# First attention: the steps of two heads placed between the matmuls of the following query blocks, and the query norm carried as one factor per token

## The chip, the cores and the metric

The kernel runs on one core of one Trainium2 chip. The metric is the device time of one execution in microseconds (us). Before the change it is 3598.67 us, the median of three runs (3596.43 to 3601.0). The profiled execution of the same kernel took 3606.35 us, with a span of 3604.6 us in the trace.

## The reference

The program is a stack of attention, recurrent and feed-forward blocks over 256 tokens of width 2048, all in float32. The change touches the first attention alone: 32 query heads and 8 key/value heads of width 64, a causal band of 128 keys, a sink per head.

```
qkv = h @ w_qkv
q, k, v = split(qkv)                       # 2048 + 512 + 512 columns
q = rmsnorm(q per head, q_gain)            # over 64 values of a head
k = rmsnorm(k per head, k_gain)
scores = einsum(q, k) * 64 ** -0.5
scores = where(0 <= qpos - kpos < 128, scores, min)
probs = softmax(concat([scores, sink]))[..., :-1]
out = einsum(probs, v)
x = x + out @ w_o
```

## The kernel before

Every weight product is cut into *units*. A unit makes a tile of 128 output features for 256 tokens: 16 steps over the 2048 input features, each with two matmuls. To keep float32 precision at the quick matmul rate, a weight tile is split into a rounded head (`w_head`, by ScalarE, L561) and the rest (`w_tail`, by VectorE, L837), and the activations are stored as head and rest side by side (`h`, 512 columns). The first matmul of a step multiplies the head of the weights with both halves (512 columns, L272), the second the tail of the weights with the heads (256 columns, L273). ScalarE copies the upper half of the bank into `lo` (L567), and VectorE adds it to the lower half (`product`, L843). A ring of four weight slots and two raw slots is filled by DMA on SyncE's queue, one tile of 1 MB a unit; the tile of unit u + 3 is split while unit u runs. Two banks, `unit0` and `unit1`, take turns.

The first attention has 24 units: 4 for keys (two heads to a tile), 4 for values, 16 for queries. In a query unit VectorE scales the product by the token norm `rstd`, ScalarE squares it, TensorE sums the squares over each head (`head_norm`, L289), ScalarE takes ln and exp for the inverse root (`head_root`, L576 and L577, each with a load of an activation table), VectorE refines it with one Newton step on 128x256 elements and writes the normed query tile to `store` (L986). The order of instructions on each engine is written out by hand, and semaphores join the engines; each engine takes its own list strictly in order.

After all 24 units the 32 heads run one by one (`attn_scores`, `attn_tile`, `turn_p`, `values`). For a head TensorE makes the scores of two blocks of 128 queries against 256 keys (L315), VectorE adds the mask (L880), takes the maximum over keys (L885) and the negative maximum with the sink (L889); ScalarE takes the exponentials with their sums (L604, L607); VectorE divides (L896 to L900); TensorE transposes four blocks (L326), ScalarE copies them (L613), TensorE multiplies by the values (L335). After each pair of heads VectorE writes the output tile, as head and rest, to `act` (L998, L999). Then the output product (`wo`, 16 units) starts; its first unit waits for all of `act`.

Of the kernel before, what the change touches and what calls it, by code (L numbers as in the profile page):

```python
# [70 lines left out]
OUTS = {"even_a": 0, "even_b": 8, "odd": 16}  # L71
NORMS = {"attn": 0, "even_kv": 20, "even_a": 22, "even_b": 30}
QS = {"attn": 0, "even_kv": 20, "even_a": 22, "even_b": 30, "odd": 38}
VTS = {"attn": 0, "even_kv": 4, "even_b": 6, "odd": 14}
# [6 lines left out]
GELUS = {"up00": 0, "up01": 16, "up02": 32, "lru_y": 48, "up10": 64, "up11": 80, "up12": 96}  # L81
GATES = {"even_a": 0, "even_b": 8, "odd": 16}
FINALS = ["wo", "down02", "lru_out", "down12", "even_out", "odd_out"]


def known(v):
    return isinstance(v, int)
# [30 lines left out]
def build(nc, t):  # L118

    ctx = ExitStack()  # L120
    with ctx:
        def sb(name, shape, dt=F32):
            return ctx.enter_context(nc.sbuf_tensor(name, shape, dt))
# [4 lines left out]
        def sem(name):  # L128
            return ctx.enter_context(nc.semaphore(name))
# [33 lines left out]
        rd = sb("rd", [P, 2, 2])  # L163
        lamb = sb("lamb", [P, 8])

        unit_bank = [pb("unit0"), pb("unit1")]
# [17 lines left out]
        p_done, t_mm, pt_done = sem("p_done"), sem("t_mm"), sem("pt_done")  # L184
        o_mm, o_read = sem("o_mm"), sem("o_read")
        gate_in, gate_th = sem("gate_in"), sem("gate_th")
        lru_a, lru_b, lru_c, lru_root, lru_d = (sem(n) for n in ("lru_a", "lru_b", "lru_c", "lru_root", "lru_d"))
# [71 lines left out]
        def _(pe):  # L259
# [89 lines left out]
            def residual(name):  # L349
                plain(name, act, (act_done, READY[name]))  # L350
# [31 lines left out]
            def trailing(g):  # L382
                if known(g) and RING <= g < 2 * RING:
                    return lambda: turn_v(g - RING, kv[:, g, :])
                n = g if known(g) and g < RING else g - RING
                return lambda: head_norm(n, halves)

            def project(i):
                for j in range(RING):
                    g = i * RING + j  # L390
                    if known(g) and g == 0:
                        first_unit()
                    else:
                        unit(i * RING + (BASE["attn"] + j), j, h, (trailing(i * RING + (j - 1)),))
            for i in range(3):
                project(i)
            with pe.Fori(3, UNITS["attn"] // RING) as i:
                project(i)
            trailing(UNITS["attn"] - 1)()


            def attn_scores(n):
                tile, lanes = n // 2, slice(HD * (n % 2), HD * (n % 2 + 1))
                scores(store[lanes, tile, :], kv[lanes, tile // 4, :], ps_s[n % 2], 20, (n - 1,) if n >= 2 else ())
            attn_scores(0)
            attn_scores(1)
            for n in range(N_Q):
                if n + 2 < N_Q:
                    attn_scores(n + 2)
                turn_p(n, n % 2)  # L410
                c = HD * (n % 2)
                values(n, ps_o[c:c + HD, 0:SEQ],
                       [kv[:, 4 + n // 8, kt * P + c:kt * P + c + HD] for kt in range(QT)], n // 2, act_done)
            residual("wo")
            ffn(0, 1)
# [136 lines left out]
        def _(a):  # L552
# [87 lines left out]

            def project(i):
                for j in range(RING):
                    u = i * RING + (BASE["attn"] + j)
                    if known(i) and i == 1:
                        step(u, j)
                        copy_vt(j, kv[:, 4 + j, :])
                    else:
                        n = i * RING + j if known(i) and i == 0 else i * RING + (j - 4)
                        step(u, j)
                        head_square(n, prod[:, :])  # L650
                        head_root(n, HD)
            project(0)
            project(1)
            repeat(a, 2, 6, project, chain)

            exps(0, 0, col(sinks, 0))

            def attn_tile(i):

                exps(i * 2 + 1, 1, col(sinks, i * 2 + 1))  # L660
                copy_pt(i * 2)
                if not (known(i) and i == N_Q // 2 - 1):
                    exps(i * 2 + 2, 0, col(sinks, i * 2 + 2))
                copy_pt(i * 2 + 1)
            repeat(a, 0, N_Q // 2 - 1, attn_tile)
            attn_tile(N_Q // 2 - 1)

# [161 lines left out]
        def _(v):  # L829
# [9 lines left out]

            def product(u, slot):  # L840

                v.wait_ge(lo_done, u + 1)
# [103 lines left out]
            v.tensor_scalar(hb[:, 1, :], lru[:, :, L_BI], 0.5, None, ALU.mult)  # L946
            v.tensor_scalar(dims[:, C_QG:C_QG + 1], dims[:, C_QG:C_QG + 1], HD ** -0.5, None, ALU.mult)
            v.tensor_scalar(dims[:, C_AQ:C_AQ + 1], dims[:, C_AQ:C_AQ + 1], HD2 ** -0.5, None, ALU.mult)
# [20 lines left out]

            def project(i):  # L970
                for j in range(RING):
                    u = i * RING + (BASE["attn"] + j)
                    product(u, j)
                    if known(i) and i == 1:
                        scaled(kv[:, 4 + j, :]).then_inc(vt_in, 1)
                        tail(u + LEAD, j + LEAD)
                        continue
                    k_tile = known(i) and i == 0
                    n = i * RING + j if k_tile else i * RING + (j - 4)
                    scaled(prod[:, :]).then_inc(norm_in, 1)  # L980
                    tail(u + LEAD, j + LEAD)
                    v.wait_ge(norm_rk, n + 1)
                    refine(rk[:, :], HD, EPS)
                    dst = kv[:, j, :] if k_tile else store[:, i * RING + (j - 8), :]
                    gain = C_KG if k_tile else C_QG
                    v.scalar_tensor_tensor(dst, prod[:, :], dims[:, gain:gain + 1], rk[:, :], ALU.mult, ALU.mult)\  # L986
                        .then_inc(q_done, 1)
                    v.wait_ge(q_done, n + 1)
            project(0)
            project(1)  # L990
            repeat(v, 2, 6, project, chain)

            def attn_front(n, slot, freed=None):
                front(n, slot, mask[:, :], 1.0, col(sinks, n), freed=freed)

            def attn_out(i):
                v.wait_ge(o_mm, i * 2 + 2)
                link(v.tensor_scalar(act[:, i, 0:SEQ], ps_o[:, 0:SEQ], 1.0, None, ALU.mult))  # L998
                v.tensor_tensor(act[:, i, SEQ:2 * SEQ], ps_o[:, 0:SEQ], act[:, i, 0:SEQ].bitcast(F32),  # L999
                                ALU.subtract).then_inc(act_done, 1)  # L1000

            def attn_tile(i, last=False):
                attn_front(i * 2 + 1, 1, None if known(i) and i == 0 else i * 2)
                back(i * 2, 0, True)
                if not (known(i) and i == 0):
                    attn_out(i - 1)
                if not last:
                    attn_front(i * 2 + 2, 0, i * 2 + 1)
                back(i * 2 + 1, 1, True)
            attn_front(0, 0)  # L1010
            attn_tile(0)
            repeat(v, 1, N_Q // 2 - 1, attn_tile, chain)
            attn_tile(N_Q // 2 - 1, True)
            attn_out(N_Q // 2 - 1)

# [82 lines left out]
            def lru_gate(m, u, slot, width, block_done):  # L1098
                v.wait_ge(lo_done, u + 1)
                v.tensor_tensor(kv[:, 7, :], act[:, m, 0:SEQ].bitcast(F32), act[:, m, SEQ:2 * SEQ].bitcast(F32),  # L1100
# [242 lines left out]
def constants():  # L1343

    q = (np.arange(QT)[None, :, None] * P + np.arange(P)[:, None, None])
    rel = q - np.arange(SEQ)[None, None, :]
    band = np.where((rel >= 0) & (rel < 128), 0.0, NEG)

# [35 lines left out]
```

## Time and profile before

| | |
|---|---|
| median of three runs | 3598.67 us |
| profiled execution | 3606.35 us, span 3604.6 us |
| TensorE busy | 3336.0 us, 93% of the span |
| VectorE busy | 2456.4 us, 68% |
| ScalarE busy | 1789.5 us, 50% |
| DMA | 561.11 MB, mean 156 GB/s |

Busy time is what the profiler saw between start and end of instructions. The granted clock tells how much of its full speed TensorE was allowed; at 0.5 a matmul of the same size takes about twice as long and is still counted busy. A busy share close to one is therefore no proof that nothing is to be gained in a stretch: the clock has to be read beside it. The chain of waits follows the work that ended last back through its releasers.

### The profile page before, as it was taken

To read this page: it belongs to the slowest core of one execution; us is meant where nothing else is said; L and a number is where in the kernel's file an instruction comes from. 1 tells how busy PE (TensorE), PEld (TensorE's weight loads), DVE (VectorE), ACT (ScalarE), POOL (GpSimd) and SP (SyncE) were. 2 spreads that over 40 slices of the span, in tenths; PEclk is the share of its full clock that TensorE was granted. 3 is DMA by queue.
4 is the path that set the end of the run, shared out by engine and by line. 5 is a ranking of instruction groups with operands and counts; after the bars stand their busy time and mean duration, and the time that the engine had idled before them with its cause. 6 is when DMAs were issued, how large, how long until landed. Compare 5 with 4: busy or idle time off the path is not lost.

```text
span 3604.6 us, 52426 instructions
## 1 busy us (share of the span) xinstructions
PE 3336.0 (93%) x17960; PEld 2820.0 (78%) x17960; DVE 2456.4 (68%) x3703; ACT 1789.5 (50%) x2281; POOL 13.1 (0%) x20
## 2 busy tenths in 40 slices
PE   8878999999999999769999999999778989999997
PEld 6744788888888888658888888888666777888876
DVE  6654577667667766777875775776455776666665
ACT  6843355445445445664554554554444554444443
POOL 1000000000000000000000000000000000000000
PEclk9965899999999999879999999999888999999998
DMA  5410355555555554235555555555223444445443
GB/s 186 144 43 0 105 186 187 181 187 184 182 187 186 182 180 150 95 117 176 197 186 187 186 179 186 185 184 186 105 84 105 152 149 141 174 164 175 173 146 122
DMA packets 83038, 561.11 MB, mean 156 GB/s; under 512 B 9728, under 2 KB 12800, under 8 KB 15872
## 3 DMA queue, kind: packets, MB, share of 16 engines
q1 hardware_dynamic: 82944, 559.87, 44.7%
q8 instruction: 57, 0.93, 0.1%
q14 instruction: 37, 0.30, 0.0%
HBM read 557.73 MB, written 2.10 MB: 155 GB/s over the span
## 4 chain that ended last, share of the span: by engine, by line
PE 70%; DVE 14%; issue 6%; ACT 6%; DMA 3%; DVEq 1%; ACTq 0%; SPq 0%
PE unit L272 42%; PE unit L273 21%; DVE w_tail L837 5%; PE o L335 2%; PE s L315 2%; PE tr L326 1%; DVE prod L843 1%; ACT w_head L561 1%; ACT L576 1%; DMA raw<-in_down 1%; ACT lo L567 1%; DMA raw<-in_lru_x 1%; ACT prt L613 1%; DVE mx L885 1%; DVE x L1024 0%
## 5 line engine op out<-in xcount | busy, mean ns | idle before, releaser
L272 PE MATMUL unit<-h,w_head 128*128 128x512 f32 x5808 | 2108.4, 406 | 40.1 <-DVE kv L1100 33.7
L273 PE MATMUL unit<-h,w_tail 128*128 128x256 f32 x5808 | 1643.3, 283 | 0.0
L272 PEld LDWEIGHTS unit<-h,w_head 128*128 128x128 f32 x5808 | 1110.9, 191 | 319.3 <-DVE kv L1100 37.0
L561 ACT ACTIVATE w_head<-raw 128x2048 fp32r<-128x2048 f32 (+1 forms) x540 | 1013.5, 1877 | 611.3 <-DMA raw<-in_up 210.8
L837 DVE TENSOR_TENSOR w_tail<-raw,w_head 128x2048 fp32r<-128x2048 f32 (+1 forms) x540 | 1209.5, 2240 | 11.5
L273 PEld LDWEIGHTS unit<-h,w_tail 128*128 128x128 f32 x5808 | 1115.4, 192 | 3.0
L272 PE MATMUL unit<-act,w_head 128*128 128x512 f32 x2560 | 910.7, 400 | 19.1 <-DVE act L854 12.9
L843 DVE TENSOR_TENSOR prod<-unit,lo 128x256 f32<-128x256 f32 x524 | 222.3, 424 | 756.2 <-ACT lo L567 750.4
L273 PE MATMUL unit<-act,w_tail 128*128 128x256 f32 x2560 | 720.6, 281 | 0.0
L272 PEld LDWEIGHTS unit<-act,w_head 128*128 128x128 f32 x2560 | 485.2, 190 | 140.6 <-DVE act L854 15.2
L273 PEld LDWEIGHTS unit<-act,w_tail 128*128 128x128 f32 x2560 | 487.7, 190 | 0.2
L567 ACT ACTIVATE lo<-unit 128x256 f32<-128x256 f32 x524 | 197.2, 376 | 316.2 <-PE unit L273 315.8
L691 ACT ACTIVATE kv<-kv,fconv 128x256 f32<-128x256 f32 x192 | 115.8, 603 | 187.3 <-DVE kv L849 187.3
L1045 DVE SCALAR_TENSOR_TENSOR kv<-kv,fconv 128x255 f32<-128x255 f32 (+1 forms) x384 | 184.8, 481 | 24.8 <-DVE kv L1045 0.9
L613 ACT ACTIVATE prt<-tr 128x512 f32<-128x512 f32 x64 | 38.3, 598 | 188.3 <-PE tr L326 188.3
L326 PE MATMUL tr<-ident,pr 128*128 128x128 f32 x256 | 59.4, 375 | 54.1 <-DVE pr L900 35.8
L607 ACT ACTIVATE pr<-pr,nm 128x256 f32<-128x256 f32 x144 | 71.5, 498 | 74.5 <-DVE nm L887 74.5
L849 DVE SCALAR_TENSOR_TENSOR kv<-prod,rstd 128x256 f32<-128x256 f32 x232 | 98.6, 425 | 9.0
L326 PEld LDWEIGHTS tr<-ident,pr 128*128 128x128 f32 x256 | 39.4, 188 | 82.5 <-DVE pr L900 41.5
L335 PE MATMUL o<-prt,kv 128*64 128x256 f32 (+1 forms) x160 | 72.3, 601 | 23.4 <-ACT prt L613 23.4
L587 ACT ACTIVATE sq<-x 128x256 f32 (+1 forms) x96 | 40.3, 419 | 107.9 <-DVE x L1024 107.9
L315 PE MATMUL s<-kv,store 64*128 64x256 f32 (+1 forms) x160 | 73.8, 622 | 9.9 <-DVE store L986 5.2
(157 smaller groups left out, 1610.4 us busy)
## 6 DMA issues: line engine op xcount, KB each, us to landing
raw<-in_up SPq DMA_DIRECT2D x192, 1024.0 KB, 4.9
raw<-in_down SPq DMA_DIRECT2D x96, 1024.0 KB, 4.9
raw<-in_odd SPq DMA_DIRECT2D x64, 1024.0 KB, 4.9
raw<-in_even_b SPq DMA_DIRECT2D x32, 1024.0 KB, 4.9
raw<-in_attn SPq DMA_DIRECT2D x24, 1024.0 KB, 4.9
raw<-in_wo SPq DMA_DIRECT2D x16, 1024.0 KB, 4.9
raw<-in_lru_y SPq DMA_DIRECT2D x16, 1024.0 KB, 4.9
raw<-in_lru_x SPq DMA_DIRECT2D x16, 1024.0 KB, 4.9
```

What stands on the lines that cost most here:

```text
L272: pe.matmul(bank[:, :], w_head[:, slot, at], src[:, k, :], start=k == 0, stop=False)
L273: last = pe.matmul(bank[:, 0:SEQ], w_tail[:, slot, at], src[:, k, 0:SEQ], start=False, stop=k == KT - 1)
L315: last = pe.matmul(bank[:, qt * SEQ:(qt + 1) * SEQ], q[:, qt * P:(qt + 1) * P], k, start=True, stop=True)
L326: last = pe.transpose(ps_t[:, kt * SEQ + qt * P:kt * SEQ + (qt + 1) * P], pr[:, slot, qt * SEQ + kt * P:qt * SEQ + (kt + 1) * P], ident[:, :])
L335: last = pe.matmul(out, v[kt], prt[:, kt * SEQ:(kt + 1) * SEQ], start=kt == 0, stop=kt == QT - 1)
L561: a.activation(w_head[:, slot, 0:width], raw[:, r, 0:width], ACT.Copy).then_inc(head_done, 1)
L567: a.activation(lo[:, slot % 2, :], unit_bank[slot % 2][:, SEQ:2 * SEQ], ACT.Copy).then_inc(lo_done, 1)
L691: a.activation(kv[:, 1 + j, :], kv[:, 0, :], ACT.Identity, scale=fconv[:, layer, tap, 2:3], bias=fconv[:, layer, tap, 3:4])\
L837: v.tensor_tensor(w_tail[:, slot, 0:width], raw[:, slot % 2, 0:width], w_head[:, slot, 0:width].bitcast(F32), ALU.subtract).then_inc(tail_ ...
L843: v.tensor_tensor(prod[:, :], unit_bank[slot % 2][:, 0:SEQ], lo[:, slot % 2, :], ALU.add)\
L849: return v.scalar_tensor_tensor(dst, prod[:, :], scale, rstd[:, :], ALU.mult, ALU.mult)
L1045: ins = v.scalar_tensor_tensor(y[:, back_by:SEQ], kv[:, 0, 0:SEQ - back_by], w, y[:, back_by:SEQ], ALU.mult, ALU.add)
```

## The change

The 4 key and 4 value units stay. Key tiles are now scaled by the product of both gains and -1/8, so that no gain has to be applied to the queries, and scores come out negated.

A query unit now has three matmuls of 256 columns a step, all into the same 256 columns of its bank (L468 to L470 of the changed kernel), so the sum of the parts needs no copy and no addition: VectorE takes the tile straight from PSUM, times `rstd` (`q_taken`, L1104). The query is not normed. Its squares are summed with the tokens on partitions, four columns for two blocks of tokens and two heads (`q_sums`), and the inverse root, 128x4 elements, multiplies the scores as one factor per token.

```diff
+            def q_part(t, k):
+                if k == 1 and t >= 2:
+                    q_turn(t - 2, 1)
+                if k == 2 and 1 <= t <= Q_TILES:
+                    q_sums(t - 1)
+                    q_scores(t - 1)
+                if k == 5 and t >= 2:
+                    q_values(t - 2)
+                if k == KT - 2 and 1 <= t <= Q_TILES:
+                    q_turn(t - 1, 0)
+            def q_unit(t):
...
+                for k in range(KT):
+                    pe.matmul(bank[:, 0:SEQ], w_head[:, slot, at], h[:, k, 0:SEQ], start=k == 0, stop=False)
+                    pe.matmul(bank[:, 0:SEQ], w_head[:, slot, at], h[:, k, SEQ:2 * SEQ], start=False, stop=False)
+                    last = pe.matmul(bank[:, 0:SEQ], w_tail[:, slot, at], h[:, k, 0:SEQ],
+                                     start=False, stop=k == KT - 1)
...
+                    q_part(t, k)
```

`q_turn` is three transposes of one head, `q_scores` the scores of both heads of a tile (queries 0 to 127 against 128 keys, queries 128 to 255 against 256; the empty quarter is left out), `q_values` both products with the values. The tile's second head is turned in the unit after next. The last two tiles' steps stand in the first two `wo` units, which now wait for each tile of `act` step by step.

ScalarE and VectorE, for each of the 16 query tiles:

```diff
+            for t in range(Q_TILES):
+                q_square(t)
+                if t:
+                    q_copy(t - 1, 1)
+                q_rooted(t)
+                g = KV_UNITS + t
+                split(BASE["attn"] + g + LEAD, g + LEAD)
+                q_exps(t, 0)
+                q_exps(t, 1)
+                q_copy(t, 0)
...
+            def q_front(t, s):
+                n = 2 * t + s
+                v.wait_ge(s_mm, n + 1)
...
+                for qt in range(QT):
+                    at = slice(qt * SEQ, qt * SEQ + (qt + 1) * P)
+                    v.tensor_tensor_reduce(pr[:, s, at], ps_s[s][:, at], mask[:, at], scale=rq[:, 2 * qt + s:2 * qt + s + 1],
+                                           scalar=nsinks[:, n:n + 1], op0=ALU.add, op1=ALU.min,
+                                           accum_out=nm[:, s, qt:qt + 1])\
+                        .then_inc((s_read, negmax_done)[qt], 1)
...
+            for t in range(Q_TILES):
+                q_taken(t)
+                q_normed(t)
+                q_front(t, 0)
+                q_front(t, 1)
+                if t:
+                    attn_out(t - 1)
+                g = KV_UNITS + t
+                tail(BASE["attn"] + g + LEAD, g + LEAD)
+                q_back(t, 0)
+                q_back(t, 1)
+            attn_out(Q_TILES - 1)
```

`q_rooted` is ln and exp on 128x4 elements, `q_normed` the Newton step on 128x4, `q_exps` the sink's and the two blocks' exponentials, `q_back` the division, `q_copy` the copy of a head's turned probabilities (384 columns; the second head's go to `lo`, which these units do not use). `tensor_tensor_reduce` adds the mask, multiplies by the token's factor and takes the minimum in one pass from PSUM. `lo_done` counts 16 fewer from here on.

TensorE in the attention, before. `s` are scores, `tr` turned probabilities, `o` the output, `pr` probabilities, `kv` keys and values:

```order
L315 MATMUL s<-kv,store 128x256 [waits s_read,q_done]
L315 MATMUL s<-kv,store 128x256
L326 MATMUL tr<-ident,pr 128x128 [waits pt_done,p_done]
L326 MATMUL tr<-ident,pr 128x128 x3
L335 MATMUL o<-prt,kv 64x256 [waits pt_done]
L335 MATMUL o<-prt,kv 64x256
L315 MATMUL s<-kv,store 128x256 [waits s_read,q_done]
L315 MATMUL s<-kv,store 128x256
```

TensorE at the end of a query unit and the start of the next, changed (`unit` is the bank of a weight product):

```order
L429 MATMUL tr<-ident,pr 128x128 [waits pt_done,p_done]
L429 MATMUL tr<-ident,pr 128x128 x2
L468 MATMUL unit<-h,w_head 128x256
L469 MATMUL unit<-h,w_head 128x256
L470 MATMUL unit<-h,w_tail 128x256
L468 MATMUL unit<-h,w_head 128x256 [waits bank_free,tail_done]
L469 MATMUL unit<-h,w_head 128x256
L470 MATMUL unit<-h,w_tail 128x256
L468 MATMUL unit<-h,w_head 128x256
L469 MATMUL unit<-h,w_head 128x256
L470 MATMUL unit<-h,w_tail 128x256
L429 MATMUL v<-ident,pr 128x128 [waits pt_done,p_done]
```

The turn of a head now stands ahead of the last step of a unit, on the same list as the matmuls of the projection.

VectorE in the attention, before:

```order
L880 SCALAR_TENSOR_TENSOR pr<-mask,s 128x512 [waits s_mm]
L885 TENSOR_REDUCE mx<-pr 128x2 [waits s_read]
L889 TENSOR_SCALAR nm<-mx,sinks 128x2 [waits dve_chain]
L896 TENSOR_TENSOR den<-den,sk 128x2 [waits exp_done]
L897 RECIPROCAL rd<-den 128x2 [waits dve_chain]
L900 TENSOR_SCALAR pr<-pr,rd 128x256 [waits dve_chain]
L900 TENSOR_SCALAR pr<-pr,rd 128x256
L880 SCALAR_TENSOR_TENSOR pr<-mask,s 128x512 [waits t_mm,s_mm]
```

VectorE for a query tile, changed, from the output of the tile before it:

```order
L1143 TENSOR_SCALAR act<-o 128x256 [waits o_mm]
L1144 TENSOR_TENSOR act<-o,act 128x256 [waits dve_chain]
L950 TENSOR_TENSOR w_tail<-raw,w_head 128x2048 [waits head_done]
L1133 TENSOR_TENSOR den<-den,sk 128x2 [waits exp_done]
L1134 RECIPROCAL rd<-den 128x2 [waits dve_chain]
L1137 TENSOR_SCALAR pr<-pr,rd 128x128 [waits dve_chain]
L1137 TENSOR_SCALAR pr<-pr,rd 128x256
L1133 TENSOR_TENSOR den<-den,sk 128x2 [waits exp_done]
L1134 RECIPROCAL rd<-den 128x2 [waits dve_chain]
L1137 TENSOR_SCALAR pr<-pr,rd 128x128 [waits dve_chain]
L1137 TENSOR_SCALAR pr<-pr,rd 128x256
L1104 SCALAR_TENSOR_TENSOR store<-unit,rstd 128x256 [waits unit_done]
```

The tail of the weight tile three units ahead, and the output of the tile before, now stand between a head's maximum and its division.

ScalarE for a query unit, before, and for a query tile, changed:

```order
L561 ACTIVATE w_head<-raw 128x2048 [waits unit_done,loaded1]
L567 ACTIVATE lo<-unit 128x256 [waits bank_free,unit_done]
L591 ACTIVATE sq<-prod 128x256 [waits norm_in]
L576 ACT_TABLE_LOAD
L576 ACTIVATE rk<-norm,lamb 128x256 [waits norm_ss]
L577 ACT_TABLE_LOAD
L577 ACTIVATE rk<-rk 128x256 [waits act_chain]
```

```order
L766 ACTIVATE prt<-tr 128x384 [waits o_mm,t_mm]
L739 ACTIVATE sq<-store 128x256 [waits bank_free]
L766 ACTIVATE lo<-v 128x384 [waits o_mm,t_mm]
L744 ACT_TABLE_LOAD
L744 ACTIVATE q_root<-norm,lamb 128x4 [waits qn_ss]
L746 ACT_TABLE_LOAD
L746 ACTIVATE q_root<-q_root 128x4 [waits act_chain]
L648 ACTIVATE w_head<-raw 128x2048 [waits unit_done,loaded0]
L752 ACTIVATE sk<-nm,sinks 128x2 [waits negmax_done]
```

The two table loads stay, their two activations shrink from 256 to 4 columns; a copy of turned probabilities stands ahead of them and the exponentials behind the split.

## Rows read from the trace of the kernel before

**Rows 1.** page: busy time of TensorE, and its granted clock by slice
```profile
PE 3336.0 (93%) x17960; PEld 2820.0 (78%) x17960; DVE 2456.4 (68%) x3703; ACT 1789.5 (50%) x2281; POOL 13.1 (0%) x20
...
PEclk9965899999999999879999999999888999999998
```

**Rows 2.** two stretches: start:end, us, busy by engine, clock, DMA share, GB/s
```profile
79.80:203.80 124.00, 100.45 (x548) 83.82 (x546) 85.30 (x131) 96.11 (x114) 0.00 (x0) 0.98 0.43 151
203.80:386.70 182.90, 158.62 (x385) 82.83 (x385) 90.69 (x254) 61.83 (x193) 0.00 (x0) 0.50 0.00 1
```

**Rows 3.** ScalarE in order of time (start, length), both ends
```profile
79.86 0.39 ACT L567 ACTIVATE lo<-unit 128x256 f32<-128x256 f32 x1 [0.25 <-PE unit L273]
...
399.68 0.38 ACT L567 ACTIVATE lo<-unit 128x256 f32<-128x256 f32 x1 [2.09 <-PE unit L273]
```

**Rows 4.** chain of waits, 300 to 320 us: shares, then start, length
```profile
by line: PE s L315 40.1%; PE o L335 29.5%; PE tr L326 21.2%; ACT prt L613 12.1%; issue 1.1%
...
301.39 1.06 PE tr L326 x4
...
307.09 1.06 PE tr L326 x4
```

**Rows 5.** ScalarE in order of time, one projection unit
```profile
153.66 1.28 ACT L576 ACT_TABLE_LOAD   x1
154.96 0.48 ACT L576 ACTIVATE rk<-norm,lamb 128x256 f32<-128x256 f32 x1
...
155.45 1.28 ACT L577 ACT_TABLE_LOAD   x1
...
156.75 0.42 ACT L577 ACTIVATE rk<-rk 128x256 f32<-128x256 f32 x1
...
161.00 1.28 ACT L576 ACT_TABLE_LOAD   x1
```

**Rows 6.** attention stretch, groups: count | busy, mean ns | idle before
```profile
L880 DVE SCALAR_TENSOR_TENSOR pr<-mask,s 128x512 f32<-128x512 f32 x32 | 22.0, 688 | 77.1 <-PE tr L326 74.9 <-PE s L315 2.2
L607 ACT ACTIVATION_READ_ACCUMULATOR pr<-pr,nm 128x1 f32 x64 | 12.0, 187 | 0.0
L604 ACT ACTIVATE sk<-nm,sinks 128x2 f32<-128x2 f32 x32 | 9.5, 295 | 47.9 <-DVE nm L889 47.9
L998 DVE TENSOR_SCALAR act<-o 128x256 f32 x13 | 5.5, 424 | 0.0
```

**Rows 7.** VectorE in order of time, one head's second half
```profile
304.24 0.15 DVE L896 TENSOR_TENSOR den<-den,sk 128x2 f32<-128x2 f32 x1
304.43 0.17 DVE L897 RECIPROCAL rd<-den 128x2 f32<-128x2 f32 x1
304.63 0.61 DVE L900 TENSOR_SCALAR pr<-pr,rd 128x256 f32<-128x256 f32 x2
```

**Rows 8.** page, costliest groups: the tail of a weight tile
```profile
L837 DVE TENSOR_TENSOR w_tail<-raw,w_head 128x2048 fp32r<-128x2048 f32 (+1 forms) x540 | 1209.5, 2240 | 11.5
```

**Rows 9.** TensorE in order of time: a pair, then three of 256 columns
```profile
1439.78 0.39 PE L272 MATMUL unit<-h,w_head 128*128 128x512 f32 x1
...
1440.13 0.28 PE L430 MATMUL unit<-act,w_head 128*128 x1
...
1440.48 0.28 PE L430 MATMUL unit<-act,w_head 128*128 x1
```

**Rows 10.** TensorE in order of time: attention between matmuls, later stage
```profile
2775.49 1.14 PE L315 MATMUL s<-store 64*128 64x256 f32 x8
...
2788.41 0.66 PE L326 MATMUL tr<-ident,pr 128*128 128x128 f32 x4 [0.27 <-DVE pr L914]
...
2794.45 1.02 PE L335 MATMUL o<-prt,store 128*128 128x256 f32 x4
```

**Rows 11.** TensorE in order of time: a wait in a later stage
```profile
2655.80 0.72 PE L326 MATMUL tr<-ident,pr 128*128 128x128 f32 x4 [2.90 <-DVE pr L900]
```

**Rows 12.** stretch of 3 us after that wait, columns as before
```profile
2657.00:2660.00 3.00, 3.00 (x11) 2.48 (x11) 0.23 (x2) 2.82 (x7) 0.00 (x0) 0.55 0.72 300
```

More of the change, by code:

```diff
@@ L395, in _ @@
[L395 to L413, printed above, removed]
@@ new lines, in q_values @@
+            def q_values(t):
+                pe.wait_ge(pt_done, 2 * t + 2)
+                if t:
+                    pe.wait_ge(act_done, t)
+                turned = (prt[:, 0:3 * P], lo[:, :, :].rearrange("p a k -> p (a k)")[:, 0:3 * P])
+                for kt in range(QT):
+                    for a in range(2):
+                        c = HD * a
+                        last = pe.matmul(ps_o[c:c + HD, kt * P:SEQ], kv[:, 4 + t // 4, kt * P + c:kt * P + c + HD],
+                                         turned[a][:, kt * SEQ:kt * SEQ + SEQ - kt * P], start=kt == 0, stop=kt == QT - 1)
+                        if kt == QT - 1:
+                            last.then_inc(o_mm, 1)
@@ L415, in _ @@
+            pe.wait_ge(act_done, KT)
+            for j in range(2):
+                wo_step(j, KT - 1).then_inc(unit_done, 1)
+            for j in range(2, RING):
+                unit(BASE["wo"] + j, j, act)
+            with pe.Fori(1, UNITS["wo"] // RING) as i:
+                for j in range(RING):
+                    unit(i * RING + (BASE["wo"] + j), j, act)
             ffn(0, 1)
@@ L652, in _ @@
[L652 to L666, printed above, removed]
+            for g in range(KV_UNITS):
+                step(BASE["attn"] + g, g % RING)
+                if g < RING:
+                    head_square(g, prod[:, :])
+                    head_root(g, HD)
+                else:
+                    copy_vt(g - RING, kv[:, g, :])
@@ new lines, in q_exps @@
+            def q_exps(t, s):
+                n = 2 * t + s
+                a.wait_ge(negmax_done, n + 1)
+                a.activation(sk[:, s, :], nm[:, s, :], ACT.Exp, bias=col(sinks, n))
+                for qt in range(QT):
+                    at = pr[:, s, qt * SEQ:qt * SEQ + (qt + 1) * P]
+                    last = a.activation(at, at, ACT.Exp, scale=-1.0, bias=nm[:, s, qt:qt + 1],
+                                        accum_out=den[:, s, qt:qt + 1])
+                last.then_inc(exp_done, 1)
@@ L1002, in attn_tile @@
[L1002 to L1013, printed above, removed]
@@ L1014, in _ @@
-            attn_out(N_Q // 2 - 1)
+            for g in range(KV_UNITS):
+                u = BASE["attn"] + g
+                product(u, g % RING, 0)
+                if g >= RING:
+                    scaled(kv[:, g, :]).then_inc(vt_in, 1)
+                    tail(u + LEAD, g + LEAD)
+                    continue
+                scaled(prod[:, :]).then_inc(norm_in, 1)
+                tail(u + LEAD, g + LEAD)
+                v.wait_ge(norm_rk, g + 1)
+                refine(rk[:, :], HD, EPS)
+                v.scalar_tensor_tensor(kv[:, g, :], prod[:, :], dims[:, C_KG:C_KG + 1], rk[:, :], ALU.mult, ALU.mult)\
+                    .then_inc(q_done, 1)
+                v.wait_ge(q_done, g + 1)
```

176 lines of the change are left out of this document (119 added, 57 removed).

## The prediction

> **What bounds the kernel now.** I read the page first. TensorE is busy 93% of the span, but the granted clock falls to 5 tenths in the third and fourth slices [rows 1]. The stretches say where: from 203.80 to 386.70 us, the 32 heads, TensorE counts 158.6 of 182.9 us as busy at a clock of 0.50, that is 1.2 GHz, while the DMA moves nothing and VectorE and ScalarE are half idle [rows 2]. In the 124 us before it, the query units, the clock is 0.98. The change lies between two points that the kernel after it has too: the end of the last value unit and the end of the second `wo` unit. ScalarE's copy of `lo` starts right behind each: 79.86 and 399.68, so 319.8 us in between [rows 3].
>
> In the heads the chain of waits is a ring of TensorE's scores, turn and values with ScalarE's copy. It comes round every 5.70 us (301.39 to 307.09) [rows 4]: 11.4 us for a tile of two heads. A query unit takes 7.34 us (153.66 to 161.00) [rows 5]. One query tile thus costs 18.7 us, and 16 of them 300.
>
> **What the change leaves on the path.** Per tile it takes away the copy to `lo`, the addition, the Newton step on 256 columns, a separate maximum and a quarter of the scores. All of that only counts through what stays. On each engine the list of a tile is fixed, so I follow tile t from the end E of its unit to the end of the next unit, which holds a turn that waits for tile t's first head.
>
> 1. TensorE makes two steps of the next unit, then turns the second head of tile t - 1. Three matmuls of 256 columns take 0.35 us, as much as the pair of today (1439.78, 1440.13, 1440.48) [rows 9]: 0.70. Three transposes, by four in 0.66 [rows 10]: 0.50. ScalarE copies 384 columns; 256 take 0.38 [rows 3], I take 0.5. Sum 1.7. The square and the sums over a head are done by then, so they cost nothing; without that cover they would add about 0.4.
> 2. Table load, ln, table load, exp. Load to activation is 1.30 both times [rows 5]; an activation on 2 columns takes 0.295 (L604) [rows 6]. 2 x 1.30 + 2 x 0.30 = 3.2. The 2 x 0.2 us that shorter activations save are in this.
> 3. Newton step on four columns: small VectorE instructions follow each other at 0.19 (304.24, 304.43) [rows 7]; four of them 0.76.
> 4. Four passes with mask, factor and minimum. This operation is not in the trace. An operation from PSUM takes 424 ns on 256 columns (L998) and 688 on 512 (L880) [rows 6]; the slope gives 0.29 for 128. A head has one of each, 0.71, and two reads of the accumulator. Read at nothing, a head costs 0.71; read as ScalarE's, 187 ns [rows 6], 1.09; if each pass went at half the pace of those rows, with the reads, 1.8. If they went at twice the pace of these rows with the read at nothing, 0.36, the other bound. I take 0.91, near the rows of the same engine. Two heads: 1.8, bounds 0.7 and 3.6.
> 5. Output of tile t - 1: two instructions of 424 ns [rows 6], 0.88.
> 6. The tail of the weight tile three units ahead, 2.24 [rows 8]. The exponentials of both heads run beside 4 to 6, behind ScalarE's split, and are done before it ends.
> 7. Division of the first head: 0.19 + 0.20, then 384 instead of 512 columns, 0.46 of 0.61 [rows 7]: 0.85.
> 8. TensorE, which has been waiting: turn 0.50 and the last step 0.35, 0.85.
>
> Sum 1.7 + 3.2 + 0.76 + 1.8 + 0.88 + 2.24 + 0.85 + 0.85 = 12.3, and 0.2 for some six handovers between engines (in the ring, seven took 1.1% of 20 us, 0.03 each, as "issue" [rows 4]): 12.5 us a tile at full clock.
>
> TensorE's own work is less: 16 steps 5.6, six transposes 1.0, scores of 768 columns 0.86 (1024 in 1.14, L315), values of 768 columns 1.5 (512 in 1.02, L335) [rows 9, 10], sums about 0.3: 9.3. So it waits about 3.2 us ahead of the turn, and behind that turn stand the last step and the next unit, whose end VectorE needs. DMA has 12.5 us for a tile that it now brings in less than 7.34, and leaves the path.
>
> **The clock.** A wait of 2.90 us ahead of a turn in a later stage [rows 11] is followed by 3 us at 0.55, at 1.2 GHz for most of them [rows 12]. That is 3 x 0.45 = 1.35 us of lost work. The waits of the query units, under 1.5 us, leave the clock at 0.98 [rows 2]. A wait of 3.2 us is with the first. What follows it (turn, last step, two steps, turn) is all on the path, so I add 1.3: 13.8 us a tile.
>
> The Trainium skill, page "TensorE: Matmul & The Clock Gate", section "HAM oscillation — how this bites in real kernels", describes this pattern, bursts of matmuls each starting throttled behind a wait for data. It speaks for 13.8 and against 12.5, and the trace agrees with it at the place of rows 11.
>
> The same collection, page "ScalarE: Activation LUTs", section "What ACT_TABLE_LOAD costs", puts a drain of 1380 ns on each switch beside the load of 1283. By it a tile would be 2.8 us longer and the time an estimated 44 us higher. Rows 5 contradict it: the activation starts 1.30 us after the load starts.
>
> **The sum.** First unit 5.6. Then 16 tiles of 13.8 = 220.8 (the sixteenth runs in the first `wo` unit), less 1.5 for the first, which has no earlier tile's copy, turn and output. Then the second `wo` unit: 15 steps 5.3, turn 0.5, values 1.5, the last two steps 0.7, in all 8.0. The third `wo` unit waits for its bank, `lo` 0.38 and an addition 0.42, which other units hid: 0.9. Sum 233.8, against 319.8: 86 us less. The profiled execution of 3606.35 becomes 3520. It lies 7.7 us above the median of 3598.67, so I forecast 3512.
>
> **Rivals.**
> - *The clock holds.* For it: over the later attention stages, slices 29 to 33, the clock is still 8 to 9 tenths [rows 1], so not every wait there lowers it for long. Against it: rows 11 and 12. 12.5 us a tile, 21 less in all: 3491.
> - *A heavier chain.* The new pass at its upper bound (1.8 us more a tile), or two falls of the clock a tile (1.3 more), or both. For it: nothing in the trace shows the pass. 15.1 to 16.9 us a tile: 3533 to 3562. The nearest rows stand against the far end.
> - *Nothing overlaps*, so that the change doesn't do what it says: unit and chain one after the other, 12.5 + 5.6 = 18.1 us a tile, 3581. Against it: the lists put 12 of 16 steps beside ScalarE's and VectorE's work.
> - *Half clock throughout, slower than before.* The small matmuls (64 rows or 64 columns) now stand in the query units. For it: at 0.50 TensorE never came back for 183 us although 87% busy [rows 2], and its matmuls there were the same scores and values. Price: steps 16 x 0.70 = 11.2; scores and values are 40.1% and 29.5% of 20 us [rows 4], for four heads and for three, so 2.0 us a head each, and for two heads three quarters of that, 3.0 + 3.0; six transposes at 0.27, 1.6; sums 0.6. TensorE is the bound with 19.4 us a tile, and 11.2 + 310.4 - 1.5 + 16.0 + 0.9 = 337.0, 17 us more: 3616. It decides from 18.3 us of TensorE work a tile. Against it: 5.6 of 9.3 us are full matmuls, as in the query units at 0.98.
>
> **How the numbers follow.** Forecast (one fall of the clock a tile) 0.50; the clock holds 0.27; heavier chain 0.17; nothing overlaps 0.02; half clock throughout 0.04. A measurement of this kernel can tell about 0.2%, 7 us, from no change. Only the last case lies on the slow side, and only the mildest forms of the last two near no change: faster 0.95, same 0.02, slower 0.03. For 8 in 10 the range takes the clock that holds, with a somewhat cheaper pass than I took, 3483, and the milder half of the heavier chain, 3545.
>
> **What would show it.** In the changed profile: `unit_done` to `unit_done` 13 to 14.5 us in the query stretch; TensorE's longest waits ahead of the transposes into `tr`, released by the division, 3 us each; a clock near 0.85 to 0.9 over the stretch; table load to activation 1.30; the new pass 0.3 and 0.4 us with a short read behind; the stretch from the last value unit to the third `wo` unit 234 us; all later stages as before. I am wrong in the mechanism if TensorE is the bound there, if ScalarE's exponentials end behind the tail, or if the wait is for the sums or for DMA; in a size alone if the passes or the clock differ.

## The result, and the profile after

The changed kernel takes 3488.05 us (median of four runs, 3487.16 to 3495.88 us), the kernel before in the same comparison 3599.84. The ratio is 0.9693, 95% interval 0.9679 to 0.9707: 3.1% faster. The forecast was 3512, with 3483 to 3545 as its range; the direction, the mechanism and the range held, and the gain was 112 us instead of 86. Some 8 of the 112 lie in stages that the change does not touch (see c_before). The profiled execution took 3488.29 us.

The page shows what answers to [rows 1]: 103 us less of busy TensorE, and the slices at 5 tenths are gone.

```profile
PE 3232.7 (93%) x18216; PEld 2795.4 (80%) x18216; DVE 2397.9 (69%) x3704; ACT 1767.3 (51%) x2265; POOL 13.1 (0%) x20
...
PEclk9889999999999998899999999999889999999998
```

The stretch that the prediction summed runs from the `lo` copy behind the last value unit to the end of the second `wo` unit. Its ends in ScalarE's rows, for [rows 3]: 80.77, and 293.08, where the copy behind the first `wo` unit starts. Both first `wo` units now end together, the second 0.3 us later, at 293.4. So the stretch is 212.6 us instead of 319.8; the forecast was 232.9.

```profile
80.77 0.38 ACT L655 ACTIVATE lo<-unit 128x256 f32<-128x256 f32 x1 [0.25 <-PE unit L278]
...
293.08 0.39 ACT L655 ACTIVATE lo<-unit 128x256 f32<-128x256 f32 x1 [1.77 <-PE unit L484]
```

Fifteen tiles of it, between the turns of their first heads, for [rows 2]: length 187.77 us, so 12.52 us a tile, clock 0.86 (the last four columns are POOL's count, the clock, the DMA share and GB/s).

```profile
96.20:283.97 187.77, 158.08 (x1096) 139.43 (x1096) 108.22 (x361) 125.48 (x270) 0.00 (x0) 0.86 0.24 85
```

VectorE in order of time (start, length), through one tile at full clock. It takes the tile out of PSUM at 160.53 and the next at 172.46:

```profile
160.53 0.42 DVE L1104 SCALAR_TENSOR_TENSOR store<-unit,rstd 128x256 f32<-128x256 f32 x1
165.19 0.16 DVE L1110 TENSOR_SCALAR q_mean<-norm 128x4 f32<-128x4 f32 x1 [4.23 <-ACT q_root L746]
...
165.85 0.41 DVE L1124 CUSTOM_DVE_ANT_0 pr<-s,mask,nsinks 128x128 f32<-128x128 f32 x1
...
166.19 0.54 DVE L1124 CUSTOM_DVE_ANT_0 pr<-s,mask,nsinks 128x256 f32<-128x256 f32 x1
...
167.45 0.42 DVE L1143 TENSOR_SCALAR act<-o 128x256 fp32r<-128x256 f32 x1
...
168.25 2.28 DVE L950 TENSOR_TENSOR w_tail<-raw,w_head 128x2048 fp32r<-128x2048 f32 x1
170.44 0.15 DVE L1133 TENSOR_TENSOR den<-den,sk 128x2 f32<-128x2 f32 x1
...
172.46 0.42 DVE L1104 SCALAR_TENSOR_TENSOR store<-unit,rstd 128x256 f32<-128x256 f32 x1 [0.23 <-PE unit L470]
```

These rows show the chain of the prediction: a hole of 4.23 us while ScalarE loads tables, then the Newton step, the four passes (0.34 and 0.46 us each from start to start), the output, the tail of the weight tile, and only then the division at 170.44 for which TensorE has been waiting. TensorE's rows at four turns, the wait in brackets:

```profile
159.59 0.55 PE L429 MATMUL tr<-ident,pr 128*128 128x128 f32 x3 [0.65 <-DVE pr L1137]
...
171.44 0.55 PE L429 MATMUL tr<-ident,pr 128*128 128x128 f32 x3 [2.86 <-DVE pr L1137]
...
184.26 0.55 PE L429 MATMUL tr<-ident,pr 128*128 128x128 f32 x3 [2.27 <-DVE pr L1137]
...
196.97 0.55 PE L429 MATMUL tr<-ident,pr 128*128 128x128 f32 x3 [0.65 <-DVE pr L1137]
```

Of TensorE's idle time that is put down to another engine in the fifteen tiles, 29.4 of 29.6 us are in front of this transpose. Five of the tiles take 11.85 us, the other ten 12.7 to 13.3 (171.44 to 184.26 is 12.82). The stretches behind the turns at 171.44 and 184.26 say why, for [rows 12]:

```profile
169.00:172.00 3.00, 0.56 (x5) 0.56 (x6) 2.86 (x9) 0.08 (x1) 0.00 (x0) 1.00 0.17 27
172.00:175.00 3.00, 3.00 (x17) 3.00 (x16) 0.66 (x2) 1.51 (x4) 0.00 (x0) 0.52 0.82 322
176.00:179.00 3.00, 3.00 (x27) 2.22 (x24) 0.89 (x5) 2.96 (x5) 0.00 (x0) 1.00 0.00 0
...
186.00:187.00 1.00, 1.00 (x7) 1.00 (x6) 0.00 (x0) 0.54 (x2) 0.00 (x0) 0.50 1.02 434
...
191.00:192.00 1.00, 1.00 (x6) 0.59 (x7) 1.00 (x7) 1.00 (x2) 0.00 (x0) 0.50 0.00 0
```

Behind the wait the clock is at 0.52 for 3 us, 1.2 GHz for nearly all of them, and back at 2.4 GHz in the third row. The last two rows are from a fall of the other kind: behind the turn at 184.26, after a shorter wait of 2.27 us, the clock is at 0.50 from 186 to 192, and the wait that follows is 0.65 (196.97).

### The profile page after: what moved, and what is told of

Same layout as the page of the kernel before. It is cut to its first block, busy times and chain, and to the rows that moved or that the text cites. A ratio compares the mean times of both kernels' runs of the same rounds, so it can differ in the third digit from the quotient of the medians.

```text
span 3486.5 us, 52830 instructions
## 1 busy us (share of the span) xinstructions
PE 3232.7 (93%) x18216; PEld 2795.4 (80%) x18216; DVE 2397.9 (69%) x3704; ACT 1767.3 (51%) x2265; POOL 13.1 (0%) x20
## 4 chain that ended last, share of the span: by engine, by line
PE 72%; DVE 14%; issue 6%; ACT 5%; DMA 2%; DVEq 1%; ACTq 0%; SPq 0%
PE unit L277 44%; PE unit L278 22%; DVE w_tail L950 5%; DVE prod L956 1%; ACT w_head L648 1%; DMA raw<-in_wo 1%; DMA raw<-in_lru_x 1%; PE o L340 1%; ACT lo L655 1%; DVE pr L1124 1%; PE s L320 1%; ACT L744 0%; PE tr L331 0%; ACT L664 0%; DVE mx L998 0%
## 5 line engine op out<-in xcount | busy, mean ns | idle before, releaser
L277 PE MATMUL unit<-h,w_head 128*128 128x512 f32 x5552 | 2004.6, 405 | 37.5 <-DVE kv L1244 33.2
L277 PEld LDWEIGHTS unit<-h,w_head 128*128 128x128 f32 x5552 | 1060.2, 191 | 300.2 <-DVE kv L1244 36.5
L278 PEld LDWEIGHTS unit<-h,w_tail 128*128 128x128 f32 x5552 | 1064.7, 192 | 2.6
L277 PE MATMUL unit<-act,w_head 128*128 128x512 f32 x2528 | 896.5, 399 | 21.4 <-DVE act L967 14.1
L278 PE MATMUL unit<-act,w_tail 128*128 128x256 f32 x2528 | 710.9, 281 | 0.0
L277 PEld LDWEIGHTS unit<-act,w_head 128*128 128x128 f32 x2528 | 477.6, 189 | 140.6 <-DVE act L967 16.6
L468 PE MATMUL unit<-h,w_head 128*128 128x256 f32 x256 | 84.1, 328 | 0.0
L1168 DVE TENSOR_TENSOR x<-x,prod 128x256 f32 (+1 forms) x160 | 68.1, 425 | 20.0 <-DVE prod L956 13.0
L470 PE MATMUL unit<-h,w_tail 128*128 128x256 f32 x256 | 77.9, 304 | 0.0
L695 ACT ACTIVATE pr<-pr,nm 128x256 f32<-128x256 f32 x80 | 40.0, 501 | 74.7 <-DVE nm L1000 74.7
L469 PE MATMUL unit<-h,w_head 128*128 128x256 f32 x256 | 77.8, 304 | 0.0
L701 ACT ACTIVATE prt<-tr 128x512 f32<-128x512 f32 x32 | 19.2, 599 | 113.2 <-PE tr L331 113.2
```

The source lines that it names most:

```text
L277: pe.matmul(bank[:, :], w_head[:, slot, at], src[:, k, :], start=k == 0, stop=False)
L278: last = pe.matmul(bank[:, 0:SEQ], w_tail[:, slot, at], src[:, k, 0:SEQ], start=False, stop=k == KT - 1)
L468: pe.matmul(bank[:, 0:SEQ], w_head[:, slot, at], h[:, k, 0:SEQ], start=k == 0, stop=False)
L469: pe.matmul(bank[:, 0:SEQ], w_head[:, slot, at], h[:, k, SEQ:2 * SEQ], start=False, stop=False)
L470: last = pe.matmul(bank[:, 0:SEQ], w_tail[:, slot, at], h[:, k, 0:SEQ], start=False, stop=k == KT - 1)
```

## The experiments

Every run is compared with the kernel before on the same chip; times in brackets are its median there.

### c_after and c_before: the two kernels again

> The changed kernel again, as the yardstick for the three beside it. Expected 3488 us, within 0.2%, with the stretch from the last value unit to the second wo unit near 213 us.

Measured: 3487.59 us (3602.16), ratio 0.969, interval 0.967 to 0.971. The stretch is 212.8 us (79.57 to 292.07, and 0.3 to the end of the second unit).

> The kernel before again, for a second trace of it. Beside the attention and the wo stage the changed kernel's trace is 15 us shorter in stages that the change does not touch. If that is chance, this trace gives other lengths for the feed-forward stages fed by DMA (177 or 181 us each), and the sum of all stages behind wo lies between 3073 and 3095 us. If the change had an effect there, this sum comes out near 3095 us again.

Measured: 3597.14 us (3597.9). The stages behind `wo`, from the first split of the feed-forward weights to the last split of all, are 3094.8 us in the first trace of before, 3083.9 in the second, 3079.2 and 3080.0 in the two traces of the changed kernel. The first 32 feed-forward tiles alone take 180.5, 177.7, 179.1 and 178.9 us, from split to split. The nine traces of the experiments below, whose kernels are the same as the changed one in these stages, give sums from 3072.8 (e_fill) to 3090.5 (e_noroot). So the 15 us are no more than these stages vary by from trace to trace. The stretch of the attention hardly varies: it is 319.7 us here (81.97 to 401.63).

### e_tail_next: the tail off the chain

```diff
             for t in range(Q_TILES):
                 q_taken(t)
+                if t:
+                    q_tail(t - 1)
                 q_normed(t)
...
-                g = KV_UNITS + t
-                tail(BASE["attn"] + g + LEAD, g + LEAD)
                 q_back(t, 0)
                 q_back(t, 1)
+            q_tail(Q_TILES - 1)
             attn_out(Q_TILES - 1)
```

`q_tail(t)` holds the two lines that are taken out.

> VectorE takes the tail of the weight tile three units ahead not between a head's maximum and its division, but at the start of the next tile, while ScalarE loads its tables. Theory 1 (the chain of a tile through ScalarE and VectorE decides, and the tail stands on it): the chain falls from 11.9 to 9.7 us, TensorE's work of 9.3 us comes near it, the tile takes 9.7 to 10.2 us instead of 12.5, the waits ahead of the turn almost go, and the time falls by 35 to 42 us, to about 3450. Theory 2 (TensorE's own work at the granted clock decides and the wait only moves): the time stays within 5 us of the changed kernel.

Measured: 3445.51 us (3602.16), ratio 0.957, interval 0.955 to 0.959; 42 us below the changed kernel beside it. TensorE at two turns, and the fifteen tiles:

```profile
172.44 0.55 PE L429 MATMUL tr<-ident,pr 128*128 128x128 f32 x3 [0.67 <-DVE pr L1137]
...
182.09 0.55 PE L429 MATMUL tr<-ident,pr 128*128 128x128 f32 x3 [0.66 <-DVE pr L1137]
```

```profile
95.24:230.34 135.10, 125.82 (x1036) 111.82 (x1036) 101.17 (x337) 117.14 (x253) 0.00 (x0) 1.00 0.32 110
```

Every tile takes 9.65 us, the wait is 0.66, and the clock is 1.00 throughout. Theory 1 holds. Its gain has two parts: 2.2 us a tile for the tail, as long as the instruction, and 0.67 for the falls of the clock that went with the long waits. TensorE's own work is 9.65 - 0.66 = 9.0 us a tile. A second measurement, the yardstick of a later comparison:

> The kernel with the tail taken in the next tile again, as the yardstick for the two beside it: 3446 us within 0.2%, 9.65 us a tile.

Measured: 3443.36 us (3600.88), ratio 0.957, interval 0.954 to 0.959.

### e_fill: the same wait without the fall of the clock

```diff
+FILL = 20
...
                 if k == KT - 2 and 1 <= t <= Q_TILES:
+                    for _ in range(FILL):
+                        pe.matmul(unit_bank[(KV_UNITS + t + 1) % 2][:, 0:SEQ], w_head[:, (KV_UNITS + t) % RING, 0:P], h[:, 0, 0:SEQ],
+                                  start=True, stop=True)
                     q_turn(t - 1, 0)
```

> Twenty matmuls of 256 columns whose result nobody reads stand ahead of each turn of a first head, in the 2.9 us in which TensorE waits there. Theory 1 (the chain decides, 11.9 us at full clock, and the falls of the clock behind each wait add 0.6 us a tile on average): the clock stays at 1.0 in the stretch, a tile takes 11.9 us, and the time falls by 8 to 10 us to 3479. Theory 2 (the falls are absorbed in the next wait, so they cost nothing): no change. If the added matmuls themselves reach over the wait, the time rises.

Measured: 3479.07 us (3602.16), 8.5 us below the changed kernel beside it; all five runs (3469.98 to 3483.29) are below all five of that kernel (3485.63 to 3491.49). Thirteen tiles take 154.05 us (108.22 to 262.27), 11.85 each; their stretch:

```profile
108.20:262.30 154.10, 148.03 (x1223) 135.02 (x1223) 93.59 (x313) 108.77 (x234) 0.00 (x0) 1.00 0.26 90
```

The clock is 1.00. The added matmuls take 2.56 us of a wait of 2.86, and the turn still waits 0.46 us behind them. So a tile at full clock is 11.85 us, and the falls cost 12.52 - 11.85 = 0.67 a tile. That is the term that I had put at 1.3. Shown here: it is the fall that costs, and work of no use in the wait buys it back.

### e_two_pass: the single pass undone

```diff
-                    v.tensor_tensor_reduce(pr[:, s, at], ps_s[s][:, at], mask[:, at], scale=rq[:, 2 * qt + s:2 * qt + s + 1],
-                                           scalar=nsinks[:, n:n + 1], op0=ALU.add, op1=ALU.min,
-                                           accum_out=nm[:, s, qt:qt + 1])\
+                    link(v.scalar_tensor_tensor(pr[:, s, at], ps_s[s][:, at], rq[:, 2 * qt + s:2 * qt + s + 1],
+                                                mask[:, at], ALU.mult, ALU.add))
+                    link(v.tensor_reduce(mx[:, s, qt:qt + 1], pr[:, s, at], AX.X, ALU.min))
+                    v.tensor_scalar(nm[:, s, qt:qt + 1], mx[:, s, qt:qt + 1], nsinks[:, n:n + 1], None, ALU.min)\
```

> The changed kernel with the single pass from PSUM undone: factor and mask in one instruction, the minimum in a second, the sink in a third, for each block. Theory 1 (the chain through ScalarE and VectorE decides): a head takes 1.6 us instead of 0.8, both heads stand on the chain, a tile 1.6 us longer, the waits ahead of the turn 4 to 4.5 us, the time 24 to 30 us longer, about 3514. Theory 2 (TensorE decides): no change beyond 5 us.

Measured: 3541.92 us (3597.9), ratio 0.984, interval 0.981 to 0.987; 54 us above the changed kernel (by the ratios to the kernel before, 0.984 against 0.969, 55), twice what I expected of theory 1. VectorE on the first block of a head and the start of the second:

```profile
184.00 0.35 DVE L1124 SCALAR_TENSOR_TENSOR pr<-s,rq,mask 128x128 f32<-128x128 f32 x1
184.38 0.29 DVE L1126 TENSOR_REDUCE mx<-pr 128x1 f32<-128x128 f32 x1
184.70 0.21 DVE L1127 TENSOR_SCALAR nm<-mx,nsinks 128x1 f32<-128x1 f32 x1
184.83 0.47 DVE L1124 SCALAR_TENSOR_TENSOR pr<-s,rq,mask 128x256 f32<-128x256 f32 x1
```

A head takes 1.93 us (184.00 to 185.93) against 0.80, so 2.3 a tile where I had assumed 1.6. The tile takes 15.56 us, 3.04 more. The rest of it, 0.8 us, I put down to the clock: the waits ahead of the turn are 2.4 to 5.1 us, and there is a stretch at 1.2 GHz around every turn, of 3.4 to 10.2 us. That is by difference; no run takes the falls out of this kernel. The direction tells for theory 1, and the longer wait cost more than itself.

### e_serial: the lean operations, one after the other

The query units hold no attention step; behind them TensorE runs

```diff
+            for t in range(Q_TILES):
+                if t + 1 < Q_TILES:
+                    q_sums(t + 1)
+                    q_scores(t + 1)
+                q_turn(t, 0)
+                q_turn(t, 1)
+                q_values(t)
```

and the other engines have two loops likewise, first what the units need (split; tail and the tile out of PSUM), then the rest of a tile.

> The changed kernel's operations, but with no attention step between the matmuls of the units: first 16 query units, then the 16 tiles one after the other, with the next tile's sums and scores ahead of a tile's turns. Theory 1 (placement is most of the gain): units at 5.8 us, 93 us; then a ring of exponentials 2.1, division 0.9, turn and copies 0.9, table loads 3.1, Newton 0.7, pass 0.8, about 9 to 9.7 us a tile at half clock, 150 us; the stretch up to the second wo unit 255 to 265 us, the time about 3535. Theory 2 (the leaner operations are the gain, placement adds little): within 10 us of the changed kernel.

Measured: 3533.30 us (3597.9), ratio 0.983, interval 0.981 to 0.986. The units, and fifteen of the tiles:

```profile
80.00:174.00 94.00, 92.61 (x774) 92.19 (x773) 44.49 (x35) 34.56 (x23) 0.00 (x0) 1.00 0.52 185
174.00:318.00 144.00, 85.71 (x390) 53.54 (x390) 70.03 (x340) 98.59 (x257) 0.00 (x0) 0.53 0.02 8
```

Units take 5.76 us each (VectorE takes them out of PSUM at 159.93, 165.69, 171.45), with TensorE busy in 92.6 of the 94 us; a tile takes 9.46 (one tile's sums start at 203.07, the next at 212.53), at a clock of 0.53. From the copy behind the last value unit (79.09) to the end of the second `wo` unit (336.6) are 257.5 us, between 319.8 before and 212.6 in the changed kernel. So of the gain of 107.2 us in the stretch, 62 are the leaner operations and 45 the placement. Up to the first scores it takes 92.6 us (to 171.68) instead of 123.9 (79.86 to 203.79), and from there 164.9 instead of 195.9: 31 us each. The numbers of theory 1 came out (9.46, 257.5, 3533), but not its headline: placement is under half. The old operations in the new places were not run, so this is the split in one order only.

### e_noroot: a tile without table loads

ScalarE's ln and exp are left out, with both table loads; the factor that VectorE works out from the mean of squares and constants is not the inverse root, so the scores are not the reference's. ScalarE's square now waits itself for the sums of the tile before.

```diff
-                a.wait_ge(qn_ss, t + 1)
-                chain.link(a.activation(q_root[:, :], ps_norm[:, 0:2 * QT], ACT.Ln, scale=1.0 / HD,
-                                        bias=lamb[:, EPS_COL:EPS_COL + 1]))
-                a.activation(q_root[:, :], q_root[:, :], ACT.Exp, scale=-0.5).then_inc(qn_root, 1)
+                pass
...
-                v.wait_ge(qn_root, t + 1)
+                v.wait_ge(qn_ss, t + 1)
```

> The changed kernel without ln and exp in the query norm and so without the two table loads a tile; VectorE works the factor out from the mean of squares and constants, so the factor is not the inverse root and the output is not the reference's. Theory 1: the chain loses 3.1 us, but the scores and the values of the tile before are then late, so 10.4 to 10.8 us a tile instead of 12.5, and the time falls by 25 to 33 us to about 3459. Theory 2 (the table loads lie beside TensorE's work and cost nothing): no change.

Measured: 3442.57 us (3597.9), ratio 0.956, interval 0.954 to 0.959; 9.63 us a tile. The table loads are on the chain, but I had put the other waits 0.8 to 1.2 us a tile too high. VectorE's waits in one tile:

```profile
173.75 0.16 DVE L1109 TENSOR_SCALAR q_mean<-norm 128x4 f32<-128x4 f32 x1 [1.32 <-PE norm L416]
...
174.70 0.41 DVE L1123 CUSTOM_DVE_ANT_0 pr<-s,mask,nsinks 128x128 f32<-128x128 f32 x1 [0.32 <-PE s L405]
...
176.71 0.43 DVE L1142 TENSOR_SCALAR act<-o 128x256 fp32r<-128x256 f32 x1 [0.33 <-PE o L442]
```

It waits for the sums, then 0.32 us for the scores and 0.33 for the values. I had the values of the tile before at 1.5 us; they take 0.80 in the changed kernel.

### The wo stage: e_wo_tail and e_wo_lead

The `wo` units behind the second took 81.1 us before, from the end of the second unit (399.68) to the last copy of `lo` (480.75), and 84.8 in the changed kernel (293.4 to 378.19). In the second traces of the two kernels they took 82.2 and 84.9 us. The prediction priced 0.9 us for the bank there, and nothing else.

```diff
             q_copy(Q_TILES - 1, 1)
+            split(BASE["wo"] + LEAD, LEAD)
             a.wait_ge(o_mm, N_Q)
...
             attn_out(Q_TILES - 1)
+            tail(BASE["wo"] + LEAD, LEAD)
```

> ScalarE splits the fourth wo weight tile before it waits for the last output of the attention, and VectorE takes its tail before it adds up the first wo unit. Theory 1 (the wo stage is fed by DMA, whose next load waits for that tail, which now comes 4 us behind the end of the second unit): the wo stage is 3 to 5 us shorter, 3484 us. Theory 2 (the stage's 4 us are chance, as in other stages fed by DMA): no difference to the changed kernel.

Measured: 3491.55 us (3602.16) against 3487.59 for the changed kernel beside it; the intervals of the ratios, 0.967 to 0.972 and 0.967 to 0.971, overlap. No gain: the fourth tile's tail started 4.8 us earlier (290.44 against 295.21), but the fifth's, at 298.95, hardly did (299.32 in the changed kernel), and the stage kept its length, 84.7 us. The second try adds this, on top of e_tail_next and of the diff above:

```diff
                     for j in range(RING):
-                        step(i * RING + (BASE[name] + j), j, last and j > 0)
+                        step(i * RING + (BASE[name] + j), j, last and j > 0 or first)
+                        if first and j < LEAD:
+                            split(BASE[name] + RING + j, j)
```

with the same order of the tails on VectorE (`first` is `wo`'s first group of four).

> On top of the kernel with the tail taken in the next tile: at the start of wo ScalarE splits the fourth tile ahead of its last wait on the attention, and in the first four wo units both engines take the split and the tail one unit earlier, the fifth tile's right behind the copy of unit 0. In four traces so far the wo stage ended 75 us behind the end of the fifth tile's tail, which comes 4.4 us behind the end of the second unit in the kernel before, and 8.3 us in the changed one. Theory 1 (DMA feeds the stage, and that tail releases it): the tail ends 3 to 4 us earlier and the stage with it, about 3442 us. Theory 2 (the 75 us are no release but TensorE's own pace): the stage keeps its length.

Measured: 3439.37 us (3600.88), ratio 0.955, interval 0.953 to 0.957. By the medians it is 4 us below the yardstick (3443.36), which the intervals cannot tell apart; the traces can. The fifth tile's tail starts at 248.86 instead of 252.85, the last copy of `lo` at 327.65 instead of 331.83, with both second units ending within 0.1 us of 246.8. From the start of that tail to that copy are 78.9 us in the kernel before, 78.9 in the changed one, 79.0 in the yardstick, 78.8 here; over all thirteen traces 78.8 to 80.1, twelve of them under 79.5. The tail frees the raw slot for which a DMA load waits; it was late because both first `wo` units end together, and the next split needs the first one's weight slot. It has the lowest median of all versions measured.

### e_out_later: the output behind the first division

```diff
-                if t:
-                    attn_out(t - 1)
                 q_back(t, 0)
+                if t:
+                    attn_out(t - 1)
                 q_back(t, 1)
```

> On top of the kernel with the tail taken in the next tile: VectorE writes the output of the tile before not ahead of the first head's division but behind it. Theory 1 (the chain still decides at 9.65 us, TensorE's work is 9.0): the division then waits for the exponentials, 0.2 us earlier than now, so 9.4 us a tile and 3 us in all. Theory 2 (9.65 us is TensorE's own bound): no change.

Measured: 3451.49 us (3600.88), ratio 0.959, interval 0.957 to 0.960; a tile takes 9.74 us instead of 9.65. Neither theory: the turn's wait does shrink, from 0.66 to 0.37 us, but the second head's division now ends behind the unit's end, and VectorE takes the next tile out of PSUM late. I saw that only in the trace, and did not vary it further.

## Why the prediction was right, point by point

**Where the gain lies.** Right: the stretch at a clock of 0.50 is gone and the tiles' steps stand in the query units. The split was not forecast; e_serial gives 62 us to the leaner operations and 45 to the placement.

**The chain of a tile.** Right in its members, and a little long in most: 12.5 us forecast, 11.85 measured from turn to turn. At full clock, from the rows above and ScalarE's:

```profile
162.08 1.28 ACT L744 ACT_TABLE_LOAD   x1
163.37 0.26 ACT L744 ACTIVATE q_root<-norm,lamb 128x4 f32<-128x4 f32 x1
163.66 1.28 ACT L746 ACT_TABLE_LOAD   x1
164.95 0.21 ACT L746 ACTIVATE q_root<-q_root 128x4 f32<-128x4 f32 x1
```

| step | forecast | measured |
|---|---|---|
| two steps, turn, copy | 1.7 | 1.55 (160.53 to 162.08) |
| two table loads, ln, exp | 3.2 | 3.11 (to 165.19) |
| Newton step | 0.76 | 0.66 (to 165.85) |
| four passes | 1.8 | 1.60 (to 167.45) |
| output | 0.88 | 0.80 (to 168.25) |
| tail | 2.24 | 2.19 (to 170.44) |
| division | 0.85 | 1.00 (to the turn, 171.44) |
| turn, last step | 0.85 | 1.02 (to 172.46) |
| sum, with handovers | 12.5 | 11.93 |

e_tail_next takes the tail away, and it counts in full: 11.85 less 2.19 is the 9.65 us found. e_noroot takes 3.11 us away and gains only 2.2 at full clock (11.85 to 9.63), since VectorE then waits for the sums, the scores and the values; e_two_pass adds to a member.

**The new pass.** Taken at 0.91 a head between bounds of 0.36 and 1.8: measured 0.80, its accumulator read 0.08 us and hidden.

**TensorE's own work.** Forecast 9.3, measured 9.0, with errors that cancel. From 159.59 on, at full clock, the sixteen steps take 6.2 us instead of 5.6 (0.36 in a row, 0.44 to 0.47 for the first behind other matmuls), the six transposes 0.54 instead of 1.0, and the values 0.80 instead of 1.5.

**The clock.** The step that failed in size is "I add 1.3: 13.8 us a tile". By e_fill the falls cost 0.67 a tile. I took each tile for itself, with one fall each. In the trace there are eleven stretches at 1.2 GHz for sixteen tiles, each behind a wait of 2.27 to 2.88 us: six of 3.4 us and five of 6.8. Behind a short one the tile takes 12.8 to 13.3 us, 1.0 to 1.4 more than 11.85, and the next wait is still 2.3 to 2.7, so the clock falls again. Behind a long one the slow work eats into the next wait (0.65 instead of 2.86, at 159.59 and 196.97): the tile takes 12.7, 0.84 more, and no fall follows. So a fall cost 1.0 us on average, and ten of the fifteen tiles had one. The two other traces that I looked through, c_after and e_wo_tail, have eleven falls as well, but there three waits of 2.25 to 2.29 us had none behind them, while one of 2.27 had. Why a fall is short or long stays open.

**How the miss adds up.** A tile took 12.52 us instead of 13.8, 1.28 less: 0.65 because the chain was shorter, 0.63 because of the clock. The fifteen tiles are 19.2 of the 20.3 us by which the stretch was shorter than forecast; its start (80.77 to 96.20, 15.4 us) was 1.6 shorter than forecast and its end (283.97 to 293.4, 9.4 us) 0.6 longer. The rival "the clock holds" gave 3491 with 12.5 us a tile, and came nearer to the time by luck: its chain was too long by what the falls, which it left out, cost.

**The table loads.** From load to activation 1.29 (162.08 to 163.37, 163.66 to 164.95). The Trainium skill's drain of 1380 ns a switch ("ScalarE: Activation LUTs", "What ACT_TABLE_LOAD costs") does not show in the changed kernel either; by it a tile would have been an estimated 2.8 us longer.

**Half clock throughout.** It did not occur: in e_tail_next the small matmuls, woven among full ones, ran at 1.00 for 135 us. In e_serial the same small matmuls by themselves ran at 0.53 for 144 us, but there TensorE also waits, up to 2.29 us at a time; which of the two holds the clock down, no run separates.

**What was missed.** The `wo` stage, 3.7 us longer, for a reason that e_wo_lead shows; I had priced only the bank at 0.9 us. So the change itself gave 319.8 - 212.6 = 107.2 us, less 3.7: 103.5, where 86 were forecast. The profiled executions differ by 118.1; nearly all of the rest lies in the stages behind `wo` and is chance, as c_before and the other traces show.

## What to carry to other kernels

When steps are woven into another loop on in-order engines, write out one turn of the loop as a chain and ask of each member whether the waiting engine needs it; here a weight tile's tail, due three units later, cost 2.2 us a tile and another 0.67 through the clock. A wait of TensorE near 3 us is dearer than it looks, yet its price is not added tile by tile, since slow work can shorten the next wait. At the end of a stage that lets DMA fall idle, look for the instruction that frees the next buffer: here it, and not the matmuls, set the end of the next stage.

## What the runs showed of the hardware

Matmuls that write the two halves of a bank's partitions start 10 ns apart. TensorE, the products with the values:

```profile
164.29 0.43 PE L442 MATMUL o<-prt,kv 128*64 128x256 f32 x1
164.30 0.43 PE L442 MATMUL o<-lo,kv 128*64 128x256 f32 x1
...
165.09 0.39 PE L468 MATMUL unit<-h,w_head 128*128 128x256 f32 x1
```

The whole, 768 columns in float32, takes 0.80 us to the next unit's matmul (164.29 to 165.09), where products on full width took 1.02 for 512 [rows 10]. The one-pass operation takes 0.34 us for 128 columns from PSUM and 0.46 for 256, where the three instructions that do the same in e_two_pass take 0.83 (184.00 to 184.83) and 1.10 (184.83 to 185.93). And matmuls of no use in the wait kept the clock at 2.4 GHz and paid: 3479.07 us in e_fill against 3487.59.
